# A transformer encoder step on one core: the order of the prologue's loads, and of the value and key products

## What is computed

```python
m = silu(c) @ w_ada + b_ada          # shift1, scale1, gate1, shift2, scale2, gate2
h = rmsnorm(x) * (1 + scale1) + shift1
q, k, v, B, C, u, g_a, g_c = split(h @ w_in)   # q 1024 columns, k 256, v 256, the others 1024 each
q, k = rmsnorm(q per head), rmsnorm(k per head)
attn = windowed attention with sinks and a relative bias table (q, [k_past, k], [v_past, v])
conv = 3-tap causal convolution of C * u
x = x + gate1 * ((sigmoid(g_a) * attn + sigmoid(g_c) * B * conv) @ w_out)
x = x + gate2 * hierarchical_moe(rmsnorm(x) * (1 + scale2) + shift2)   # 64 experts, top 2
# further outputs: the newest 128 rows of k and v and two rows of C * u, for both groups
```

## Time and profile before

| what | value |
|---|---|
| median of three runs | 1600.86 us |
| the profiled execution's own time | 1597.34 us |
| its span, first to last instruction | 1595.9 us |
| busy: PE, DVE, ACT, POOL | 83%, 30%, 15%, 24% of the span |
| mean granted TensorE clock | 0.938 of full speed |
| DMA | 479.24 MB, mean 300 GB/s |

### The profile page before, as it was taken

How to read it: one execution, slowest core, us unless ns; L and a number is a source line. 1 busy time by engine, 2 the same in 40 slices (tenths; PEclk the granted TensorE clock), 3 DMA queues, 4 the chain that set the end, 5 groups by cost and what they waited for, 6 DMA issues and landing times.

```text
span 1595.9 us, 21998 instructions
## 1 busy us (share of the span) xinstructions
PE 1317.6 (83%) x7914; PEld 763.5 (48%) x7915; DVE 479.3 (30%) x966; ACT 237.2 (15%) x460; POOL 376.6 (24%) x582
## 2 busy tenths in 40 slices
PE   3479999999999966898989887887778878778883
PEld 2478899888987532333333333333333333223331
DVE  1535644656443443112212121121112112111214
ACT  2313332333321110101010000000000000000000
POOL 2536554455530001111111111111111111111111
PEclk9689999999999977999999999999999999999997
DMA  9534433233316446999996999999999999999984
GB/s 327 186 93 121 134 116 110 80 125 125 121 31 229 174 184 254 423 426 427 412 426 263 427 426 425 426 426 426 422 424 408 426 421 414 415 418 418 411 323 169
DMA packets 112162, 479.24 MB, mean 300 GB/s; under 512 B 15452, under 2 KB 67836, under 8 KB 87788
## 3 DMA queue, kind: packets, MB, share of 16 engines
q1 hardware_dynamic: 95312, 457.85, 71.1%
q0 software_dynamic: 13248, 13.59, 2.9%
q10 hardware_dynamic: 3580, 7.51, 1.3%
HBM read 483.18 MB, written 24.46 MB: 318 GB/s over the span
## 4 chain that ended last, share of the span: by engine, by line
PE 53%; DMA 38%; DVE 4%; issue 2%; SPq 1%; ACT 1%; ACTq 0%; POOL 0%; POOLq 0%; DVEq 0%
DMA ws<-in_w_up 26%; PE ps L739 20%; PE ps L953 16%; DMA ws<-in_w_down 9%; PE ps L965 6%; PE ps L867 3%; DMA ws<-in_w_in 2%; PE ps L836 1%; PE ps L821 1%; PE ps L702 1%; PE ps L769 1%; PE ps L937 1%; DMA ws<-yc_dram 1%; DVE arena L1306 1%; PE ps L750 1%
## 5 line engine op out<-in xcount | busy, mean ns | idle before, releaser
L953 PE MATMUL ps<-ws,arena 128*64 128x512 f32 x1920 | 469.8, 646 | 116.3 <-DMA ws<-in_w_gate 75.3
L953 PEld LDWEIGHTS ps<-ws,arena 128*64 128x64 f32 x1920 | 166.4, 148 | 418.3 <-issue 418.3
L739 PE MATMUL ps<-ws_r 128*128 128x274 f32 x1600 | 281.2, 294 | 9.8 <-issue 9.8
L385 POOL TENSOR_TENSOR held<-small 128x1 f32<-128x1 f32 x225 | 46.9, 208 | 861.6 <-DMA yc_dram<-arena,cur 290.5
L965 PE MATMUL ps<-ws,arena 128*64 128x512 f32 x960 | 212.6, 595 | 34.0 <-DMA ws<-in_w_down 28.1
L739 PEld LDWEIGHTS ps<-ws_r 128*128 128x128 f32 x1600 | 233.1, 191 | 14.1 <-issue 12.9
L1511 DVE TENSOR_TENSOR misc<-misc,ps 128x512 f32<-128x512 f32 x33 | 22.7, 688 | 590.8 <-PE ps L953 590.8
L739 PE MATMUL ps<-arena_r,ws_r 128*128 128x274 f32 x800 | 167.4, 291 | 0.0
L965 PEld LDWEIGHTS ps<-ws,arena 128*64 128x64 f32 x960 | 76.2, 137 | 149.7 <-issue 110.7
L739 PEld LDWEIGHTS ps<-arena_r,ws_r 128*128 128x128 f32 x800 | 127.7, 191 | 0.0
L571 POOL TENSOR_TENSOR ws_r<-ws,ws_r 128x1024 fp32r<-128x1024 f32 x48 | 120.0, 2501 | 3.8
(11 more groups left out here) (271 smaller groups left out, 1122.2 us busy)
## 6 DMA issues: line engine op xcount, KB each, us to landing
ws<-in_w_gate SPq DMA_DIRECT2D x59, 2048.0 KB, 17.6
ws<-in_w_up SPq DMA_DIRECT2D x59, 2048.0 KB, 18.2
ws<-in_w_down SPq DMA_DIRECT2D x59, 2048.0 KB, 19.2
ws<-in_w_ada SPq DMA_DIRECT2D x12, 2048.0 KB, 8.7
ws<-in_w_in SPq DMA_DIRECT2D x48, 512.0 KB, 3.8
merged<-in_w_gate SPq DMA_DIRECT2D x3, 2048.0 KB, 20.2
arena<-in_w_up SPq DMA_DIRECT2D x3, 2048.0 KB, 18.9
arena<-in_w_down SPq DMA_DIRECT2D x3, 2048.0 KB, 15.3
```

Of the source, the lines that this page charges most:

```text
L385: return eng.tensor_tensor(cell, epsc, epsc, ALU.add)
L739: last = nc.tensor.matmul(ps[:, 2 * buf + h, 0:HALF], w[:, k, :], x[:, k, HALF * h:HALF * h + HALF], start=(k == 0 and part == 0), stop=(k ...
L953: last = nc.tensor.matmul(ps[CAP * e:CAP * e + CAP, m, :], xT[c][:, k, CAP * e:CAP * e + CAP], weights[e][:, k, :], start=(k == 0), stop=( ...
```

## The change

- SP issues the four w_ada chunks right behind the x tiles; the waits for `rows_ld` and `state_ld` are gone. wv is loaded before wk.
- The table's store to DRAM is issued by POOL and no longer by ACT. The spread is in two transfers: heads 0 and 1 first (256 KB), heads 2 to 15 (1792 KB) behind the first four `halve`; the first back-load waits for the first part alone.
- POOL makes the high and the low part of wv, and the low part of hT's tile 1. ACT no longer rounds wk before the modulation; it does so after the five tiles. DVE makes the low part of wk last, after the low parts of hT, which now stand between the modulations of the tiles.
- PE does the value tiles 0 to 3 first, each as its low part is there, in four PSUM banks; then both key projections, with the first sum of squares after the fourth k of the second; then value tile 4 and the second sum of squares.
- The keys' copies to the other partitions are issued by SP, and PE no longer waits for them; POOL's copy `kcur` does. `halve(4)` and `halve(5)` stand before that copy instead of behind it.
- Turn 0 of the loop is written out ahead of a loop over the turns 1 to 7, on PE, ACT and DVE. In it, PE transposes the key rows after the fifth w_ada chunk, DVE copies them into the space of tB, ACT issues their store, and DVE waits for the store before it writes tB.

```diff
@@ SP
-            sp.wait_ge(rows_ld, 16 * 9)
-            sp.wait_ge(state_ld, 64)
             for c in range(4):
                 sp.dma_start(wstage[c], w_ada[:, :, 512 * c:512 * c + 512]).then_inc(ada_ld[c], 16)
+            sp.dma_start(wv, w_in[:, :, C_V:C_V + 256]).then_inc(wv_ld, 16)
             sp.dma_start(wk, w_in[:, :, C_K:C_K + 256]).then_inc(wk_ld, 16)
-            sp.dma_start(wv, w_in[:, :, C_V:C_V + 256]).then_inc(wv_ld, 16)
...
             sp.wait_ge(v_mm, NTT)
+            sp.wait_ge(proj_mm, 2)
             sp.dma_start(wstage[0], w_ada[:, :, 4 * 512:5 * 512]).then_inc(ada_ld[0], 16)
+            for a in range(2):
+                sp.wait_ge(kn_rdy, a + 1)
+                for h in range(2):
+                    sp.dma_start(kTd[HD * (1 - h):HD * (1 - h) + HD, 2 * a + h, :],
+                                 kTd[HD * h:HD * h + HD, 2 * a + h, :]).then_inc(kdup_st, 16)
+            sp.wait_ge(v_rdy, NTT)
...
@@ POOL
+            def bias_spread(h0, h1):
+                src = bass.AP(bias_dram, h0 * NREL + (P - 1), [[NREL, h1 - h0], [-1, P], [1, 2 * P]])
+                pool.dma_start(biasq_dram.ap()[h0:h1], src).then_inc(biasrow_st, 16)
+
+            pool.wait_ge(brow_rdy, 1)
+            pool.dma_start(bias_dram.ap(), biasrow[0:NH, :]).then_inc(biasrow_st, 16)
             pool.wait_ge(biasrow_st, 16)
-            pool.dma_start(biasq_dram.ap(), bass.AP(bias_dram, P - 1, [[NREL, NH], [-1, P], [1, 2 * P]])).then_inc(biasq_st, 16)
-            pool.wait_ge(biasq_st, 16)
+            bias_spread(0, 2)
+            pool.wait_ge(biasrow_st, 32)
...
+            pool.wait_ge(ada_mm, 1)
+            pool.wait_ge(wv_ld, 16)
+            pool.tensor_copy(wv_hi, wv).then_inc(wv_high, 1)
+            pool.wait_ge(wv_high, 1)
+            pool.tensor_tensor(wv_lo, wv, wv_hi.bitcast(F32), ALU.subtract).then_inc(wv_low, 1)
+            pool.wait_ge(hT_high, 2)
+            low_part(nc.gpsimd, 1).then_inc(hT_lowp, 1)
             pool.wait_ge(ada_mm, 2)
             for i in range(4):
                 halve(i, 0, i + 1)
+            bias_spread(2, NH)
+            pool.wait_ge(proj_mm, 2)
+            for i in (4, 5):
+                halve(i, 0, i + 1)
             pool.wait_ge(kdup_st, 16 * 4)
-            pool.wait_ge(kn_rdy, 2)
             pool.wait_ge(v_rdy, NTT)
             pool.wait_ge(state_ld, 64)
             pool.tensor_copy(kcur[:, :], kTd[:, 0, :]).then_inc(kcur_rdy, 1)
             pool.tensor_copy(vcur[:, :, :], vT[:, :, 0:HD]).then_inc(kcur_rdy, 1)
-            pool.wait_ge(proj_mm, 2)
-            for i in (4, 5):
-                halve(i, 0, i + 1)
...
@@ PE
+            def v_rows(t):
+                c0, rows, _ = TILES[t]
+                pe.wait_ge(*((hT_low, 1), (hT_lowp, 1), (hT_low, 2), (hT_low, 3), (hT_low, 4))[t])
+                if t == 4:
+                    pe.wait_ge(v_rdy, 3)
+                for k in range(KT8):
+                    for part, (x, w) in enumerate(((hT_hi, wv_hi), (hT_hi, wv_lo), (hT_lo, wv_hi))):
+                        last = nc.tensor.matmul(ps[0:rows, V_BANK[t], 0:256], x[:, k, c0:c0 + rows], w[:, k, :],
+                                                start=(k == 0 and part == 0), stop=(k == KT8 - 1 and part == 2))
+                last.then_inc(v_mm, 1)
...
             pe.wait_ge(zero_rdy, 10)
-            pe.wait_ge(hT_low, NTT)
+            pe.wait_ge(wv_low, 1)
+            for t in range(4):
+                v_rows(t)
+            pe.wait_ge(hT_low, NTT - 1)
             pe.wait_ge(kv_low, 1)
             project(wk_hi[:, :, 0:P], wk_lo[:, :, 0:P], 0)
-            project(wk_hi[:, :, P:2 * P], wk_lo[:, :, P:2 * P], 1)
-            pe.wait_ge(sq_rdy, 1)
-            sumsq()
...
-            pe.wait_ge(kdup_st, 16 * 4)
-            pe.wait_ge(v_rdy, NTT)
...
+            project(wk_hi[:, :, P:2 * P], wk_lo[:, :, P:2 * P], 1, [(3, k_sumsq, 0)])
+            v_rows(4)
+            k_sumsq(1)
...
                 ada(None, 0, 5, 0, 16 * j + 32)
+                if isinstance(j, int):
+                    k_rows_out()
...
+            turn(0)
+            with pe.Fori(1, NJ) as j:
+                turn(j)
@@ ACT
-            act.wait_ge(ada_mm, 1)
-            act.wait_ge(wk_ld, 16)
-            nc.scalar.activation(wk_hi, wk, ACT.Copy).then_inc(kv_high, 1)
...
-            act.wait_ge(wv_ld, 16)
-            nc.scalar.activation(wv_hi, wv, ACT.Copy).then_inc(kv_high, 1)
+            act.wait_ge(wk_ld, 16)
+            nc.scalar.activation(wk_hi, wk, ACT.Copy).then_inc(kv_high, 1)
...
+            for t in range(4):
+                v_out(t)
             square(a_free, 1)
             root(1)
-            v_out(0)
-            v_out(1)
             square(b_free, 1)
-            v_out(2)
+            v_out(4)
             act.wait_ge(kn_rdy, 1)
             root(2)
-            v_out(3)
-            v_out(4)
@@ DVE
-            kv_rest(1, wk, wk_hi, wk_lo)
...
+            modulated(0)
+            modulated(1)
+            low(0)
+            modulated(2)
+            modulated(3)
+            low(2)
+            modulated(4)
+            low(3)
+            low(4)
+            dve.wait_ge(kv_high, 1)
+            V.tensor_tensor(wk_lo, wk, wk_hi.bitcast(F32), ALU.subtract).then_inc(kv_low, 1)
```

More of the change, by code:

```diff
@@ L77, in __call__, with enter @@
         self.eng.wait_ge(self.sem, self.base + self.n)
-    def enter(self, i, per):
-        self.start, self.per = self.base + self.n, per
+    def enter(self, i, per, first=0):
+        self.start, self.per = self.base + self.n - first * per, per
         self.base, self.n = self.start + i * per, 0
@@ L402, in window, with token_cols, low_part @@
             return SEQ, 0, WIN + DEC
+        def token_cols(t):
+            c0, rows, _ = TILES[t]
+            return slice(c0 - PAD if t in (0, 4) else c0, c0 + rows)
+        def low_part(eng, t):
+            c = token_cols(t)
+            return eng.tensor_tensor(hT_lo[:, :, c], hT[:, :, c], hT_hi[:, :, c].bitcast(F32), ALU.subtract)
+        V_BANK = (6, 7, 4, 5, 4)
         @block.sync
@@ new lines, in k_sumsq, with k_rows_out @@
+            def k_sumsq(a):
+                pe.wait_ge(sq_rdy, a + 1)
+                if a == 0:
+                    pe.wait_ge(v_rdy, 2)
+                else:
+                    pe.wait_ge(ss_used, 1)
+                sumsq()
+            def k_rows_out():
+                pe.wait_ge(kn_rdy, 2)
+                pe.wait_ge(ss_used, 3)
+                for i, (c0, rows) in enumerate(((SEQ - WIN, WIN), (SEQ + WIN, DEC))):
+                    for q in range(NKV):
+                        r = slice(HD * (q % 2), HD * (q % 2) + HD)
+                        at = 2 * HD * i + HD * (q // 2)
+                        last = nc.tensor.transpose(ps[0:rows, S_BANK[0][q % 2], at:at + HD], kTd[r, q, c0:c0 + rows], ident[r, r])
+                        if q >= 2:
+                            last.then_inc(outT_mm, 1)
@@ L755, in _ @@
             pe.wait_ge(zero_rdy, 10)
-            pe.wait_ge(hT_low, NTT)
+            pe.wait_ge(wv_low, 1)
+            for t in range(4):
+                v_rows(t)
+            pe.wait_ge(hT_low, NTT - 1)
             pe.wait_ge(kv_low, 1)
             project(wk_hi[:, :, 0:P], wk_lo[:, :, 0:P], 0)
-            project(wk_hi[:, :, P:2 * P], wk_lo[:, :, P:2 * P], 1)
-            pe.wait_ge(sq_rdy, 1)
-            sumsq()
-            pe.wait_ge(kv_low, 2)
-            for t, (c0, rows, _) in enumerate(TILES):
-                if t >= 2:
-                    pe.wait_ge(v_rdy, t - 1)
-                for k in range(KT8):
-                    for part, (x, w) in enumerate(((hT_hi, wv_hi), (hT_hi, wv_lo), (hT_lo, wv_hi))):
-                        last = nc.tensor.matmul(ps[0:rows, 4 + t % 2, 0:256], x[:, k, c0:c0 + rows], w[:, k, :],
-                                                start=(k == 0 and part == 0), stop=(k == KT8 - 1 and part == 2))
-                last.then_inc(v_mm, 1)
-                if t == 2:
-                    pe.wait_ge(sq_rdy, 2)
-                    pe.wait_ge(ss_used, 1)
-                    sumsq()
@@ L777, in _ @@
-            pe.wait_ge(kdup_st, 16 * 4)
-            pe.wait_ge(v_rdy, NTT)
-            for i, (c0, rows) in enumerate(((SEQ - WIN, WIN), (SEQ + WIN, DEC))):
-                for q in range(NKV):
-                    last = nc.tensor.transpose(ps[0:rows, 4 + i, HD * q:HD * q + HD], kTd[0:HD, q, c0:c0 + rows],
-                                               ident[0:HD, 0:HD])
-                last.then_inc(outT_mm, 1)
-            with pe.Fori(0, NJ) as j:
+            project(wk_hi[:, :, P:2 * P], wk_lo[:, :, P:2 * P], 1, [(3, k_sumsq, 0)])
@@ L786, in step, with turn @@
+            v_rows(4)
+            k_sumsq(1)
+            def turn(j):
                 def step(i, buf, free, count, hooks=()):
@@ L799, in scores @@
                     k0, _, n = window(t)
+                    if isinstance(j, int) and t == 0:
+                        pe.wait_ge(outT_rdy, 2)
```

(13 more changed lines are left out.)

54 lines of the change are left out of this document (24 added, 30 removed).

## The result

The changed kernel took 1582.93 us (median of four runs, 1579.26 to 1584.58), the kernel before beside it 1600.97. The ratio is 0.9885 with a 95% interval of 0.9866 to 0.9904: faster by 1.0 to 1.3%, 18 us by the medians. I had forecast 1569.2 us with a range of 1562 to 1581. The direction was right, the saving (31.7) was overstated by 13.7, and the measured time lies above the range.

What follows compares the result with a forecast made beforehand. PE and DMA bound nine tenths of the span; the front waited for key weights, elementwise work and key copies. A new timeline put step 2 of turn 0 at 93.6 instead of 125.27: 1600.86 - 31.7 = 1569.2 us, range 1562 to 1581.

Steps and rivals of the forecast that it cites:

- The mark: Start of step 2 of turn 0, after which both kernels do the same work; forecast 93.6 us against 125.27.
- The gain is given back later: Rival: something after step 2, such as POOL in turn 0, is late by what was saved; 1600.9 us, chance 0.03.
- slower: Rival: clock at half from value tile 1 to step 2, 6 us slower, 1607 us; chance 0.02.
- The loads: Front: four w_ada chunks behind x at 5.4 each, plus 1.3 for the table; last chunk at 32.8 instead of 43.5.
- Value weights and the first tile: Front: wv lands at 36.5, POOL's rounding and subtraction end at 43.3, the first tile's low part at 44.5.
- PE: Value tiles 0 to 3 from 44.5 to 57.4, with nothing charged for wk's low part; then first key projection, 6.2.
- the clock stays low through the values: Rival: gaps between value tiles keep PE at half clock for four tiles; plus 9.9, 1579.1 us, chance 0.14.
- The key norm: Before turn 0: 6.4 from the sum of squares' end to normed keys; PE idles 1.8, step 0 starts at 76.4.
- T + 8: 8 us after T, the first key projection's end, forecast at 63.6; normed keys were put at T + 10.4.
- DVE and POOL hold each other up: Rival: wk's low part comes 5.5 late, or the keys' copies eat their cover; 1574.7 us, chance 0.10.
- The small loads late: Rival: early chunks delay ACT's row loads by 11.7, so chunk matmuls end 5.9 later; 1575.1 us, chance 0.08.
- The copies and the other costs at nothing: Charged zero as covered: keys' copies on SP (6 us of cover), fifth w_ada chunk (7), halves, router loads, key-row store.

Runs made afterwards that it cites:

- e2: Changed kernel with the spread and first load-back of table heads 0 and 1 moved behind POOL's first four halves; 1570.85 us, ratio 0.9817.
- e4: Changed kernel with SP's waits for row and state loads put back before the first w_ada chunk; 1584.95 us, ratio 0.9902.
- e3: Changed kernel with the whole table (16 heads, 2048 KB) spread where it spreads two heads; 1584.96 us, ratio 0.9908.
- e1: Changed kernel with halve(4) and halve(5) moved back behind POOL's copy of the keys; 1578.05 us, ratio 0.9847.
- e12: e11 with value tile 3 moved from ahead of the key products to behind them; 1571.18 us, ratio 0.9808.
- e6: Changed kernel with PE waiting again for the keys' four copies before turn 0; 1591.98 us, ratio 0.9941.
- e5: Changed kernel with PE's old order, both key projections ahead of the value tiles; 1584.95 us, ratio 0.9892.
- e11: Changed kernel with the edits of e1 and e2 together; 1571.18 us, ratio 0.9810.

## Why the prediction was wrong, point by point

*The mark.* Right: the saving was decided before step 2 of turn 0, 18.0 there and 18.0 in the medians. "The gain is given back later" and "slower" did not happen. All three signs that I had named against the sum came: the last chunk after 37 (39.9), clock 0.50 beyond 52 us (until 56.2), and POOL's copies not done at 100 (99.4 to 100.6).

*The loads: the step that failed first.* I had put the last chunk at 32.8, from "x is in by 10", 5.4 per chunk and 1.3 for the table's bytes. It came at 39.9, 7.1 later. e2 gives the split: without the table it is 34.8, so the table cost 5.1 where I had charged 1.3, which is 3.8 of the miss; the other 3.3 is w_ada itself, at 34.8 where my sum without the table has 31.5. Of that, 2.1 arose at the first chunk, which landed at 17.5 in e2 where my sum has 15.4 (18.9 in the changed kernel). The idle 41 GB/s of 10 to 12 us that I wanted to fill was there, but in the window ahead of it the engines of the kernel before were full with the loads of ACT and POOL, and those now run beside w_ada:

```profile
8.00:10.00 2.00, 0.34 (x1) 0.18 (x1) 0.23 (x1) 0.18 (x1) 0.86 (x2) 1.00 1.13 283
```

e4 shows the net of the early issue: 1 us. The forecast's 391 GB/s was a price from a window without small transfers.

The figure that should have warned me stood in the earlier trace rows. I took "about 6" between the ends 4.5 and 16.2 "since its bytes are few". It was 12.9, near the upper end. (The back-load, the other half of my 1.3, was issued only at 38.9.) The packet records of the trace show how so few bytes hold up a chunk. The spread of two heads is 64 packets of 4096 B, from 30.3 to 38.0 us, and never more than two of them are under way at once; in e3, with sixteen heads, up to 15 are. At 28 to 30 us about 190 packets of w_ada (2048 B each) start per us. From 36 to 40 only 34 are left, at most two at once, beside 1153 of 1024 B of the loads that stand behind it in the same queue. So most of the 16 DMA engines had gone on to the next loads, and the chunk waited for two. On these the two transfers take turns, packet by packet: one of 162 ns of the spread, then one of 85 ns of w_ada. My estimate from these records, 32 spread packets of 162 ns on each of the two engines, is 5.2 us of delay, and e2 measured 5.1. The records name no engine, so that it is one engine per head is what I infer. What is open is e3: the other fourteen heads cost 3.2 more. A spread of the same two heads over more engines was not tried. The Trainium skill, "DMA: Bandwidth & Descriptors" ("Queues, rings and completion order"), says of a copy on SP's or ACT's queue that it is split across up to 16 rings, not always all of them, and ("Why a DMA increments its semaphore by 16 and not by 1") that the count is full only when each of the engines that took part has its data landed. The packets agree: the chunk counted as landed at 39.9, 0.5 behind the end of its last packet (39.4).

*Scale and shift.* Forecast 2.0 after the last chunk's matmuls (36.2 to 38.2), measured 2.0 (43.2 to 45.18). DVE's low part of wk was in that path, as read.

*Value weights and the first tile.* Forecast 6.3 from the modulation to the first value product, measured 5.5. DVE's low part started at 47.83 and ended at 50.6, 1.1 after POOL's subtraction of 4.51 (44.94 to 49.45): the whole instruction was waited for, as I took from the longest row. But it was not alone: PE itself transposed the last tile until 50.4.

*PE.* The four value tiles took 14.0 (forecast 12.9), without gaps, at a granted clock of 0.50 until 56.2 and 1.00 from there, and the first key projection followed at once (64.75). So the rival "the clock stays low through the values", to which I gave 0.14, did not come, and my zero for the low part of wk stands.

*The key norm: the step that failed second.* "From its end to normed keys it took 6.4 before" was right for DVE alone. I had seen in the first part that DVE and POOL take turns, and priced it there, yet did not ask what POOL would do at T + 8. The change moves `halve(4)` and `halve(5)` to just that time. It was 4.9 us, and the half clock behind PE's longer idle time cost 1.2 in the sum of squares and 1.7 in step 0. e1 returns 5.3 at the mark. My rival "DVE and POOL hold each other up" had the mechanism and the price (5.5) and the wrong place. With 0.10 on it, and the loads late by 7 in no rival, the range could not hold a case with both, and both came.

*The sum of the misses.* Chunk 7.1, scale to value tiles -0.8, values 1.1, key norm 4.9, clock 1.2 and 1.7, and 1.5 less in step 1, the chunk and the key transposes: 13.7.

*The small loads late.* In part this rival came: the state rows reached PE at 15.18 instead of 11.12, but the input's transposes began at 20.89 instead of 19.77, which nothing waited for.

*The copies and the other costs at nothing.* Right in the changed kernel: the last copy landed in time, the scores did not wait. The fifth w_ada chunk had its cover there, but e12 shows how thin it was.

*What each part of the change gave*, at the mark: the keys' copies off the path 8.3 (e6), the last chunk 3.6 earlier, the low part of wk out of the modulation's way 3.1, the value lead 3.2 (e5). That is 18.2 for 18.0, closer than the parts are known: in e6 and e5 the last chunk was 1.0 and 0.5 earlier than in the changed kernel, and with that they read 9.3 and 3.7, a sum of 19.7. Of the 3.6, 1.0 is the early issue (e4). e3 puts the split of the table at 3.1 (the chunk at 43.1 and 39.9), so the two overlap or are rough by half a microsecond.

## What to carry to other kernels

A transfer that is waited for by its completion is as late as the slowest engine that carries it, so price what runs beside it by the packets that it puts on one engine and not by its bytes: here 256 KB cost 5.1 us, nearly what I would have given 2 MB (5.4). When work is moved onto POOL, list DVE's instructions with two SBUF inputs that fall in the same microseconds, at the new time and not at the old. And before a large reordering, ask what stands under the long chain afterwards: the value products had been the cover of the key norm, and a lead of 11.7 us for PE was worth 3.2, by my estimate some 7 without POOL's halves in the way.

## What the runs showed of the hardware that I had not expected

- The 256 KB spread of two heads never had more than two packets under way, and on those engines its packets of 4096 B and w_ada's of 2048 B took turns, 162 and 85 ns.
- 256 KB in two heads took 12.7 to 12.9 us to land beside w_ada and 7.7 to 8.3 with little beside it; 2048 KB in sixteen took 16.0 to 16.2 and 9.5.
- Large loads issued among small ones moved 254 to 295 GB/s with the engines at a share above 1.0, against 381 to 393 once the small ones were done, from 16 to 26 us.
- After an idle 6.8 us, four 274-column matmuls took 2.19 us instead of 1.09 to 1.19 (granted clock 0.50), and the 48 behind them 7.95 instead of 6.2. After an idle 1.95 the four took 1.19, 1.73, 1.80 or 2.00 in four executions, at a granted clock of 1.00 in the first (e11) and 0.56 to 0.65 in the others. After an idle 2.50 in e12 the clock was still 1.00. So a short gap costs the clock sometimes.
- DVE's four two-input instructions of the key norm took 1.84 us alone, 3.57 (e5) and 6.70 beside POOL's two halves.
